# Deferring the K/V norm in a hybrid decoder step: projecting x times the norm weight before 1/rms is known

## The reference, cut to what matters

```python
def rms_norm(x, g):
    xf = x.astype(jnp.float32)
    y = xf * lax.rsqrt(jnp.mean(xf * xf, axis=-1, keepdims=True) + RMS_EPS)
    return (y * g.astype(jnp.float32)).astype(x.dtype)
...
    out = y @ w_out
    return x + rms_norm(out, norm_post), hr, hi          # end of the state-space layer
...
def shared_kv(x, kv_norm, w_kv):
    bsz, seq_len, _ = x.shape
    kv = rms_norm(x, kv_norm) @ w_kv
    return kv.reshape(bsz, seq_len, 2, N_HEADS, HEAD_DIM)
...
    h = rms_norm(x, norm_pre)                            # attention layer, another norm weight
    proj = h @ w_in                                      # three groups of q, and z
```

## Time and profile before

| | |
|---|---|
| median of 3 runs | 1545.5 us (1543.17 to 1546.32) |
| profiled execution, its own time | 1544.77 us |
| its span in the trace | 1543.0 us |
| mean granted TensorE clock | 0.947 of full speed |
| PE busy | 1365.5 us, 88% |
| DVE, ACT, POOL busy | 634.1, 510.3, 522.9 us (41%, 33%, 34%) |

### The profile page before, as it was taken

The page is one execution under the profiler, slowest core; times in us unless marked ns, Lnnn a source line. Parts: engine busy times, 40 slices in busy tenths (PEclk is TensorE's granted clock), DMA queues, the critical chain, the costliest instruction groups (busy, mean ns, idle before and its releaser), DMA issues. The chain is left out here.

```text
span 1543.0 us, 29855 instructions
## 1 busy us (share of the span) xinstructions
PE 1365.5 (88%) x12197; PEld 1290.5 (84%) x12197; DVE 634.1 (41%) x1010; ACT 510.3 (33%) x889; POOL 522.9 (34%) x310
## 2 busy tenths in 40 slices
PE   5588888978988999999997996799889999999893
PEld 3578878977988999999997995799878887889693
DVE  5866648996921221221220005561234333443314
ACT  4223332414542222222221123232345544545221
POOL 0312222330014344344342331133356555554130
PEclk9789999998999999999999998899999999999897
DMA  5466884431123333333332231134756666563311
GB/s 128 74 128 128 140 118 103 126 111 48 48 71 97 109 92 105 109 94 104 109 99 64 86 92 40 43 86 149 222 181 193 226 193 222 178 219 99 95 54 56
DMA packets 271635, 178.84 MB, mean 116 GB/s; under 512 B 64848, under 2 KB 260136, under 8 KB 271040
## 3 DMA queue, kind: packets, MB, share of 16 engines
q1 hardware_dynamic: 270912, 144.18, 35.7%
q10 hardware_dynamic: 640, 33.49, 6.0%
HBM read 157.36 MB, written 53.77 MB: 137 GB/s over the span
## 5 line engine op out<-in xcount | busy, mean ns | idle before, releaser
L109 POOL TENSOR_TENSOR w_lo<-raw,w_hi 128x1024 fp32r<-128x1024 f32 x168 | 409.0, 2436 | 816.8 <-ACT w_hi L104 609.6
L161 PE MATMUL acc<-act_hi,w_hi 128*128 128x256 f32 x1728 | 353.9, 286 | 30.4 <-POOL w_lo L109 24.0
L161 PE MATMUL acc<-act_lo,w_hi 128*128 128x256 f32 x1728 | 351.8, 285 | 0.0
L161 PE MATMUL acc<-act_hi,w_lo 128*128 128x256 f32 x1728 | 351.3, 285 | 0.0
L161 PEld LDWEIGHTS acc<-act_hi,w_hi 128*128 128x128 f32 x1728 | 271.8, 191 | 32.9 <-issue 26.4
L104 ACT ACTIVATE w_hi<-raw 128x1024 fp32r<-128x1024 f32 x156 | 164.8, 1057 | 343.0 <-PE acc L161 289.6
L161 PEld LDWEIGHTS acc<-act_lo,w_hi 128*128 128x128 f32 x1728 | 271.6, 191 | 0.0
L161 PEld LDWEIGHTS acc<-act_hi,w_lo 128*128 128x128 f32 x1728 | 271.4, 190 | 0.0
L1277 DVE SCALAR_TENSOR_TENSOR sig<-acc,vec,sig 128x520 f32<-128x520 f32 x16 | 12.2, 760 | 293.4 <-PE acc L161 293.4
L1821 PE MATMUL acc<-act_hi,w_hi 128*128 128x256 f32 (+1 forms) x512 | 112.9, 302 | 8.9 <-ACTq L2076 8.7
L1821 PE MATMUL acc<-act_lo,w_hi 128*128 128x256 f32 (+1 forms) x512 | 105.1, 287 | 0.0
(11 more groups left out here) (298 smaller groups left out, 2062.6 us busy)
## 6 DMA issues: line engine op xcount, KB each, us to landing
raw<-a_w_glu SPq DMA_DIRECT2D x64, 512.0 KB, 4.0
s_kv<-cache_kv ACTq DMA_DIRECT2D x8, 4088.0 KB, 16.3
raw<-a_w_in SPq DMA_DIRECT2D x32, 512.0 KB, 4.3
raw<-b_w_in SPq DMA_DIRECT2D x32, 512.0 KB, 4.5
raw<-a_w_out SPq DMA_DIRECT2D x16, 512.0 KB, 3.6
raw<-w_kv SPq DMA_DIRECT2D x16, 512.0 KB, 3.9
k_rows<-cache_kv SPq DMA_DIRECT2D x32, 256.0 KB, 7.4
v_rows<-cache_kv SPq DMA_DIRECT2D x16, 512.0 KB, 6.6
```

What stands on the lines that cost most here:

```text
L109: pool.tensor_tensor(self.mem.wl[s][:, :, :], self.mem.raw[s][:, :, :], self.mem.wh[s][:, :, :].bitcast(F32), ALU.subtract).then_inc(self. ...
L161: ins = nc.tensor.matmul(mem.acc[a][:, 256 + lo:256 + hi], w[s][:, k, :], x[:, k0 + k, lo:hi], start=first and k == 0 and i == 0, stop=las ...
```

## The change

- The K/V product takes `x * norm weight` as its input, without 1/rms. ACT makes the high part (a Copy with the norm weight as its scale), DVE the low part, within `residual`, behind each addition to `xT`. The sum of squares goes on beside it.
- `first_tiles` of K/V moves from `mixer` into `residual`, ahead of the barrier; PE sums the squares of tile f-1 between its k-blocks.
- The root and the inversion for the K/V norm now both stand at the end of `residual`.
- `kv_tile` multiplies by 1/rms where it copied.
- `warm`: ACT does a square root of 8 columns ahead of the last two squares of each `residual`, so that the activation table is loaded there. This also affects `b_out`.
- The distance tables, which overlap the norm's buffers, load two q tiles in, behind the last K/V tile, and no longer at t = 13.

```diff
+    def warm(self, act):
+        act.activation(self.root[:, 0:8], self.mem.cst[:, :], ACT.Sqrt)
...
             if nxt:
                 nxt.split_hi_first(act, dn, units * DT)
+            nm.warm(act)
             for m in range(DT - 2, DT):
                 square(m, m % 2, m // 2)
             nm.take_root(act)
             if next_norm:
                 for f in range(DT):
                     act.wait_ge(added, 2 * f + 2)
+                    act.activation(mem.acth[:, f, :], mem.xT[:, f, :], ACT.Copy,
+                                   scale=mem.vec[:, next_gains + f:next_gains + f + 1]).then_inc(next_norm.act_hi, 1)
                     next_norm.square(act, f, f % 2, mem.xT[:, f, :])
                 next_norm.take_root(act)
...
                 pe.wait_ge(nm.rooted, 1)
-                for f in range(DT):
-                    next_norm.add(pe, f, f % 2, f == 0, f == DT - 1)
+
+                def ready(f):
+                    pe.wait_ge(next_norm.act_lo, f + 1)
+                    if f:
+                        next_norm.add(pe, f - 1, (f - 1) % 2, f == 1)
+                nxt.start(pe)
+                nxt.first_tiles(pe, mem.acth, mem.actl, ready)
+                next_norm.add(pe, DT - 1, (DT - 1) % 2, last=True)
...
+            def low(f):
+                v.wait_ge(next_norm.act_hi, f + 1)
+                v.scalar_tensor_tensor(mem.actl[:, f, :], mem.xT[:, f, :],
+                                       mem.vec[:, next_gains + f:next_gains + f + 1],
+                                       mem.acth[:, f, :].bitcast(F32), ALU.mult, ALU.subtract).then_inc(next_norm.act_lo, 1)
...
                 v.tensor_tensor(mem.xT[:, f, :], mem.xT[:, f, :], nm.tmp[f % 2][:, :], ALU.add).then_inc(added, 1)
+                if next_norm and f:
+                    low(f - 1)
             v.wait_ge(added, 2 * DT)
+            if next_norm:
+                low(DT - 1)
+                next_norm.invert(v)
+                v.wait_ge(next_norm.act_lo, DT)
...
             def tables():
-                sp.wait_ge(nm.act_lo, 2 * DT)
+                sp.wait_ge(kv_ready, 2 * DT)
...
                 if t == 13:
+                    small_tables()
+                if t == Q0 + 2:
                     tables()
-                    small_tables()
...
-            dn.start(pe)
-            dn.first_tiles(pe, *xk, lambda k: pe.wait_ge(nm.act_lo, k + 1))
...
-                v.tensor_copy(to.rearrange("p (c j) -> p j c", j=L), x[:, 0:SEQ].rearrange("p (j c) -> p j c", j=L))
-                v.tensor_copy(kvs[:, m // DT, f, :], x[:, SEQ:TOK]).then_inc(dn.acc_free[m % 2], 1)
+                v.tensor_tensor(to.rearrange("p (c j) -> p j c", j=L), x[:, 0:SEQ].rearrange("p (j c) -> p j c", j=L),
+                                nm.rstd[:, 0:SEQ].rearrange("p (j c) -> p j c", j=L), ALU.mult)
+                v.tensor_tensor(kvs[:, m // DT, f, :], x[:, SEQ:TOK], nm.rstd[:, SEQ:TOK],
+                                ALU.mult).then_inc(dn.acc_free[m % 2], 1)
...
-            nm.invert(v)
-            nm.apply(v, V_KV, 0)
...
-            nm.apply_hi(act, 0)
             for t in range(2 * DT):
                 dn.split_hi(act, t + 2, t % 2, t // 2 + 1)
                 if t < DT:
-                    nm.apply_tile_hi(act, DT, t, DT)
+                    nm.apply_tile_hi(act, DT, t, 0)
```

More of the change, by code:

```diff
@@ L1292, in residual @@
 def residual(nc, mem, name, dn, ten_w, units, xh, xl, gains, o_at, norm_at, natural=False, next_norm=None,
-             nxt=None):
+             next_gains=None, nxt=None):
     ot, _ = mem.at(f"{name}_o", [P, DT, TOK], o_at)
@@ L1401, in ssm_out @@
     residual(nc, mem, "a_out", mem.a_out, ten["a_w_out"][0, :, :], 2, mem.yh, mem.yl, V_APOST, mem.acth_at, mem.glu_end,
-             next_norm=mem.kv_norm, nxt=mem.proj)
+             next_norm=mem.kv_norm, next_gains=V_KV, nxt=mem.proj)
 BQ = 3 * DT
```

## The result

The changed kernel takes 1548.76 us (median of 20 runs, 1544.77 to 1554.14); the kernel before, in as many runs beside it, 1544.49 us (1541.25 to 1548.19). The medians differ by 4.3 us. The ratio estimated from all these runs is 1.0031, with a 95% interval from 1.0021 to 1.0042: slower by 4.8 us (3.2 to 6.5), where +3.5 was forecast. The profiled execution took 1545.98 us, only 1.2 more than that of before, at the same mean clock of 0.947. So the answer has to be looked for at the place of the change, not in the difference of two spans.

What follows compares the result with a forecast made beforehand. PE was taken as the bound, so time changes only where it stands still or runs at low clock. 2.9 + 0.35 + 0.3 - 0.05 = +3.5 us: 1548.3 us profiled, 1549.0 median, range 1545.0 to 1551.0.

Steps and rivals of the forecast that it cites:

- Step 1: End of `a_out`: table load ahead of the squares costs 1.5 us, a clock fall in PE's sums 1.4; +2.9.
- Rival 1: PE's clock holds through the 3.3 us gap at `a_out`'s end; total +2.1, 1547.6 us; chance 0.20.
- Step 2: First K/V tiles: PE starts 16.4 us earlier; DVE needs about 2.05 us for a feature tile.
- Step 3: First K/V tiles and sums: PE is the bound, 19.75 us; 9.9 us gained, 8.9 counting the last sum.
- Step 4: Behind the first tiles: root, inversion (3.40 us) and barrier (0.25) now follow in sequence; SP enters `mixer` at 974.3.
- Step 5: Tile 2's weights: the 4.0 us landing loses its cover; tile 2 0.35 us later, PE idle 12.2 us.
- Step 6: Tile 2 onward: low clock +0.3 us; PSUM multiplication and later tables zero; `b_out`'s earlier table load saves 0.05.
- Rival 2: Tile 2's loads are not held by the barrier and come under the first tiles; -3.2, 1542.3 us; chance 0.08.
- Rival 3: One more stall: ACT after the moved load, 1550.3 us, or POOL blocking K-tile multiplications, 1551.4; chance 0.10.

Runs made afterwards that it cites:

- e2: The kernel before with only the small early root (early table load) added; ratio 1.0015 to the kernel before.
- e4: The changed kernel with SP's weight loads of tiles 2 and 3 issued ahead of the barrier; ratio 1.0020 to the kernel before.
- e3: The kernel before with K/V copies turned into multiplications by 1/rms and the tables loaded late; ratio 1.0002 to the kernel before.
- e5: The changed kernel with loads of tiles 2 and 3 and tile 2's split ahead of the barrier; ratio 0.9976 to the kernel before.
- e1: The changed kernel without the small early root, so the table load stands behind the last two squares; ratio 1.0018 to the kernel before.
- e7: The changed kernel with only the small early root moved ahead of the two prefetched splits; ratio 1.0015 to the kernel before.
- e6: e5 with the small early root moved ahead of the two prefetched splits, hiding the table load; ratio 0.9969 to the kernel before.
- e8: Norm deferred as in the changed kernel, but first tiles left behind the barrier, inversion beside them, no early table load; ratio 1.0007 to the kernel before.
- e9: e6 with ACT's first copy of turned K rows put ahead of a high part at t = 2; 1540.24 us, ratio 0.9946 to the kernel before.

## Why the prediction was right, step by step, and what its size leaves open

The mechanism was right; a reading ahead of it was not. The longest wait of L177, 8.7 us, was that of the program's start, and the one ahead of the K/V tiles was 6.94 us. Nothing in the sum used it.

**Step 1** (table load, +2.9 taken): the mechanism was right and the size 2.45. The order's part was 1.52 (1.5), the clock's 0.92, not 1.4: the first four of the sums' matmuls still ran at full clock (0.90 us at 1.00 in the stretches above). Rival 1, that the clock holds, occurred behind the same gap in e2. The fall differs between executions, as the prediction supposed.

**Step 2** (first tiles early): L177 starts 8.03 us behind the root of `a_out`; by my steps it is 8.01 (948.95 less 940.94). DVE needs 2.07 us for a feature tile; 2.05 was said.

**Step 3** (PE the bound, 19.75 us): from 952.96 to the last sum's start at 972.33 it is 19.37 us, with no wait for `act_lo` between. The pace at full clock is 2.32 us (2.38). Counted from the split and with the last sum, PE is done 6.8 us sooner than before in spite of step 1's 2.45 (973.37 - 938.79 = 34.58 us against 978.62 - 937.25 = 41.37), so 9.2 without it; 8.9 was said.

**Step 4** (root, inversion, barrier): from the root's end at 974.24 to SP's issue at 978.16 it is 3.92 us; 3.68 was said. The barrier took 0.48 of it, from the inversion's end at 977.68, and not 0.25.

**Step 5** (landing exposed): 982.48 - 978.16 = 4.32 us (4.0), then 3.63 to PE (3.62); PE idles 12.74 us (12.2). This was the step that decided the sign, and e4 shows it: with the loads ahead of the barrier, 4.23 of those 4.32 us are gone. Tile 2 is 0.50 us later than step 1 alone makes it; 0.35 was said.

**Step 6** (the rest): the multiplication and the tables cost nothing that can be told (e3). PE resumed at the low clock: from the start of tile 2 to the matmul behind the 4.99 us stall it took 13.47 us, and 12.97 before (981.62 to 994.59), so 0.50 (0.3 was said). Most of it is made up by attention, where 0.06 is left. In `b_out` the root follows PE's sum by 0.04 instead of 0.11 us, so 0.07 is gained (0.05). The timeline there, against the earlier trace rows:

```profile
1513.18 0.84 ACT L537 ACTIVATE b_out_post_root<-aux,cst 128x256 f32<-128x256 f32 x2 [1.23 <-PE aux L525]
```

**Rival 2** (loads not held) is refuted by SP's issue at 978.16, behind the inversion's end. Its price was right, though: e4 and e5 do by hand what it supposed, and tile 2 in e5 comes 3.8 us earlier than before (it said 3.2). **Rival 3**: ACT's small root starts 0.01 us behind the table load (939.87 + 1.28 = 941.15), and its squares follow at once, so there is no second stall. The drain that the Trainium skill gives in "ScalarE: Activation LUTs", section "What ACT_TABLE_LOAD costs", does not show at this place either. Of the 16 multiplications only that at 986.56 ran wholly beside a POOL operation, and it took 1.12 us; the others end before POOL starts or within 0.1 us of it (1009.46 and 1009.37), so they do not test the blocking. The one agrees with "SBUF — State Buffer", section "Who interferes with whom", of the Trainium skill: one operand lies in PSUM, and it is not stretched, while the scaling beside POOL, with its operands in SBUF, takes 2.71.

**The size.** By the marks the change costs 2.9 us: 2.45 from step 1, 0.50 from step 5, 0.06 left of step 6's clock, less 0.07; forecast were 2.9, 0.35, 0.3 and 0.05. The times say 4.8 (3.2 to 6.5), so the forecast of 3.5 lies in the interval and the marks just below it. That the median of 1549.0 was forecast and 1548.76 measured is partly luck: the kernel before came out at 1544.49, and the forecast had set out from 1545.5. The profiled execution, forecast at 1548.3, took 1545.98.

Is a further cost hidden in the clock? Each timed run lists its own mean clock: the changed kernel's runs have 0.9433 on the mean (standard error 0.0006), the kernel before, in 87 runs beside the experiments, 0.9455 (0.0002). Much of such a difference can lie at the place of the change, under an idle PE. The view by stretches from ACT's split to attention, for the kernel before, and then for the changed one, followed by its 12.74 us of idling:

```profile
937.25:1108.52 171.27, 143.22 (x1094) 137.51 (x1095) 78.30 (x86) 56.60 (x87) 48.12 (x21) 0.93 0.34 96
```

```profile
938.79:1113.07 174.28, 141.61 (x1094) 137.46 (x1095) 72.10 (x78) 56.75 (x88) 48.48 (x21) 0.90 0.32 93
973.37:986.11 12.74, 0.00 (x1) 0.03 (x1) 7.27 (x6) 3.48 (x5) 2.91 (x3) 0.64 0.29 82
```

Read in stretches of 2 us, the clock stands at 0.5 for 23.9 us of this part before and for 34.1 after, and 9.2 us of the latter are in that one idle gap. These 10.2 us at half the clock lower the mean of a 1545 us run by 0.0033, which is more than the 0.0022 measured, and what they cost is in the marks already. In e1, e4 and e7 the same part holds 30.7 to 30.8 us at 0.5, worth 0.0022, and their runs lie 0.0020 to 0.0027 below the kernel before. So for these kernels the clock gives no ground for a further term. (It is not a full account of the clock: the runs of e5, e6, e8 and e9 lie 0.0012 to 0.0021 lower than this part of their traces makes them, with errors of 0.0005 to 0.0008.) What the times have beyond 2.9 us (0.3 to 3.6) stays open. One trace of each kernel can't settle it: where the clock falls and how long it stays low differ between executions (22.4 us for the first tiles in e1, 21.3 in the changed kernel), and the timed runs hold all such cases. The same is open for e4, whose time was higher than its marks.

## What to carry to other kernels

When work moves ahead of a barrier, list the transfers that it covered. A prefetch that stays behind loses its cover, and here the whole gain (9 us of PE's work moved into waits) went into one landing, a split and the inversion; moved along, with the table load hidden, the same idea gave 4.8 us. A table load "taken early" pays only where the engine is idle: ahead of an operation that others wait for, it cost its full length here, 1.52 us with the small root, and more where the clock fell. And ask of each engine's order what stands ahead of the one operation that the bounding engine waits for, as the 4 us of e9 show.

## What the runs showed that was not expected

- The same 3.25 us gap on PE let the clock fall within the next sums in one execution (2.94 us for them) and not in another (2.02).
- Executions of one kernel on one chip spread by 14 and 18 us (before: 1542.33 to 1556.08 on one, 1540.96 to 1559.3 on another), so that 12 runs gave intervals of some 3 us to either side. The mean clock spreads with them: over the 215 timed runs, compared within each kernel on its chip, 0.97 us goes with each 0.001. It was 0.938 in the execution of e7 that took 1555.91 us, 0.947 in that of the changed kernel that took 1545.98.
- A product of a PSUM and an SBUF operand with a strided output costs DVE no more than the copy did: 1.15 us on the mean for 512 columns, as for the copy.
- The stay at 0.5 from the start of the first tiles was 3.3 us in the kernel before and some 6 us in e1, e2 and e7. Only e2 had the longer gap ahead of the sums, so that gap does not explain it; the cause stays open.
